# Deeper hi/lo rings, GpSimd alone on the ungated low halves, and expert cells fetched before expert rows, in a one-core PEER inference step

## What is computed

```python
q = (xb @ w_q).reshape(PEER_BLOCK, PEER_HEADS, 2, D_KEY // 2)      # 8 heads, two half keys of 128
s = jnp.einsum('thpc,pnc->thpn', q, sub_keys)
sv, si = lax.top_k(s, PEER_TOPK)                                   # 16 of 128, for each half
cand = sv[:, :, 0, :, None] + sv[:, :, 1, None, :]                 # 256 sums
best, flat = lax.top_k(cand, PEER_TOPK)                            # 16 of 256
idx = i1 * N_KEYS + i2                                             # one of 16384 experts
gate = jax.nn.softmax(best, axis=-1)
act = gelu(einsum('thkd,td->thk', u_tab[idx], xb))
coef = gate * act
out = einsum('thk,thkd->td', coef, v_tab[idx])                     # then x + out and a final RMSNorm
```

## Time and profile before

| | |
|---|---|
| median of 3 runs | 1560.5 us (1558.67 to 1567.8) |
| the profiled execution | 1566.55 us, its span 1564.7 us |
| queries | 501.8 to 575.5 us of the span |
| ungated blocks | to 829.4 |
| gated blocks | to 1112.2 |
| value stage | to 1556.0 |
| tail | to 1564.7 |
| TensorE matmul busy | 1372.6 us, 88% |
| VectorE, ScalarE, GpSimd busy | 64%, 43%, 23% |
| one pick on VectorE (line 1934, 128 x 1024), mean of 62 | 1278 ns |

### The profile page before, as it was taken

The page is one execution under the profiler, slowest core; times in us unless marked ns, Lnnn a source line. Parts: engine busy times, 40 slices in busy tenths (PEclk is TensorE's granted clock), DMA queues, the critical chain, the costliest instruction groups (busy, mean ns, idle before and its releaser), DMA issues.

```text
span 1564.7 us, 24623 instructions
## 1 busy us (share of the span) xinstructions
PE 1372.6 (88%) x8950; PEld 1177.7 (75%) x8950; DVE 1000.1 (64%) x1850; ACT 667.7 (43%) x1492; POOL 359.3 (23%) x284
## 2 busy tenths in 40 slices
PE   6999865998796998899999999999999159799997
PEld 5987632787434988889999999999877147677775
DVE  4556788444523248999327777777677147677776
ACT  4432042231002454344456666666555125455554
POOL 1110131001100015475661000000334743222210
PEclk9999676999888999999999999999999679999998
DMA  6430200000132334444546444444577158888864
GB/s 219 136 120 28 115 16 1 1 1 28 31 161 91 121 100 130 133 139 145 167 140 195 125 126 127 129 126 125 163 257 255 41 195 263 276 272 278 277 217 135
DMA packets 117612, 219.26 MB, mean 140 GB/s; under 512 B 31649, under 2 KB 32161, under 8 KB 116513
## 3 DMA queue, kind: packets, MB, share of 16 engines
q1 hardware_dynamic: 106272, 184.78, 37.5%
q0 software_dynamic: 11264, 33.60, 6.5%
HBM read 207.64 MB, written 10.42 MB: 139 GB/s over the span
## 4 chain that ended last, share of the span: by engine, by line
PE 41%; DVE 10%; POOL 7%; DMA 4%; issue 4%; ACT 3%; SPq 0%; ACTq 0%; DVEq 0%; POOLq 0%
PE ph L1702 9%; PE ph L1703 8%; PE ph L1704 8%; PE acc L1772 4%; POOL RT L1590 4%; PE pg L1753 4%; PE acc L1774 4%; PE acc L1773 4%; DVE ohx L1934 3%; POOL lo L1579 2%; ACT hi L1612 2%; DMA raw<-in_v 2%; DVE lo L1787 1%; DVE hid L1812 1%; DVE hid L1809 1%
## 5 line engine op out<-in xcount | busy, mean ns | idle before, releaser
L1612 ACT ACTIVATE hi<-raw 128x512 fp32r<-128x512 f32 x544 | 341.6, 632 | 483.0 <-PE acc L1774 203.2
L1787 DVE TENSOR_TENSOR lo<-raw,hi 128x512 fp32r<-128x512 f32 x448 | 313.7, 709 | 209.8 <-ACT hi L1612 208.2
L1702 PE MATMUL ph<-xh,hi 128*128 128x320 f32 x1152 | 366.4, 318 | 27.4 <-DVE lo L1787 20.8
L1703 PE MATMUL ph<-xl,hi 128*128 128x320 f32 x1152 | 358.1, 311 | 0.0
L1704 PE MATMUL ph<-xh,lo 128*128 128x320 f32 x1152 | 357.9, 311 | 0.0
L1772 PE MATMUL acc<-hi,ch 128*128 128x512 f32 x512 | 207.6, 405 | 74.8 <-DVE cl L1945 74.7
L1702 PEld LDWEIGHTS ph<-xh,hi 128*128 128x128 f32 x1152 | 218.5, 190 | 33.7 <-DVE lo L1787 22.9
L1703 PEld LDWEIGHTS ph<-xl,hi 128*128 128x128 f32 x1152 | 218.6, 190 | 0.0
L1704 PEld LDWEIGHTS ph<-xh,lo 128*128 128x128 f32 x1152 | 218.1, 189 | 0.0
L1774 PE MATMUL acc<-lo,ch 128*128 128x512 f32 x512 | 201.9, 394 | 0.0
L1773 PE MATMUL acc<-hi,cl 128*128 128x512 f32 x512 | 201.7, 394 | 0.0
(11 more groups left out here) (360 smaller groups left out, 1890.9 us busy)
## 6 DMA issues: line engine op xcount, KB each, us to landing
raw<-in_uT SPq DMA_DIRECT2D x256, 256.0 KB, 2.7
raw<-in_v SPq DMA_DIRECT2D x256, 256.0 KB, 3.1
wraw<-in_w_in SPq DMA_DIRECT2D x30, 512.0 KB, 3.5
raw<-in_w_q SPq DMA_DIRECT2D x32, 256.0 KB, 2.8
wo<-in_w_out SPq DMA_DIRECT2D x4, 1024.0 KB, 10.7
h_scratch<-act_s SPq DMA_DIRECT2D x128, 32.0 KB, 2.5
sth<-in_state_h SPq DMA_DIRECT2D x1, 2048.0 KB, 7.6
out_hgrn_s<-stn SPq DMA_DIRECT2D x1, 2048.0 KB, 6.9
```

The lines of the kernel that those rows point to most:

```text
L1612: act.activation(wide(hi[n % 4]), wide(raw[n % 4]), ACT.Copy).then_inc(t_hi, 1)
L1702: pe.matmul(o, hi[s][:, k], xh[:, c], start=begin, stop=False)
L1703: pe.matmul(o, hi[s][:, k], xl[:, c], start=False, stop=False)
L1787: dve.tensor_tensor(wide(lo[n % 4]), wide(raw[n % 4]), wide(hi[n % 4]), ALU.subtract).then_inc(lo_v, 1)
```

## The change

It does these things:

- `hi` and `lo` have 8 buffers each (`RING`); `raw` keeps 4. The four row buffers `vbuf` are no longer memory of their own, but the first 4096 columns of `hid`, free once the value stage has read its first 16 blocks (GpSimd waits for `c_lo` 16).
- ScalarE's `high` runs ahead by six tiles in place of two (`high(2m + 6)`, `high(UA + 2b + 6)`); in the value stage two blocks ahead.
- GpSimd makes all low halves of the ungated stage; `share()` is gone from the retrieval.
- ScalarE's loop over blocks is written in another order: `hidden(b-1)` comes first, then the scaling of the one-hots, then two `high`. The store of `act_s` moves from SP to ScalarE (`spill`), behind the two `high`.
- GpSimd fetches all 64 cells first and then the 64 sets of rows. `ACC_AT` is `38 + 4k/3`: three in four blocks, from block 38 to block 122. The steps of the tail move two blocks or one block later.
- The exponentials, the transposes of the picks and the loops of TensorE are placed by steps of 8 tiles in place of 4.

```diff
-        NPICK, EARLY = 64, 16
+        NPICK = 64
-        EXP_AT, PICKED = NA // 2 - 4, NA // 2 - 3
-        ACC_AT = {10 + 5 * k // 3: k for k in range(NPICK)}
+        RAW, RING = 4, 8
+        EXP_AT, PICKED = NA // 2 - 4, NA // 4 - 2
+        ACC_AT = {38 + 4 * k // 3: k for k in range(NPICK)}
...
-        vbuf = [big_mem.sb(f"vbuf{r}", [P, D]) for r in range(4)]
+        vbuf = [hflat[:, D * r:D * r + D] for r in range(4)]
...
-                    if n % 2 and 0 <= b < NBLK:
-                        sp.wait_ge(hs_done, b + 1)
-                        sp.dma_start(hs_dram[b], act_s[b % 4][:]).then_inc(hs_out[b % 4], 16)
...
-                    if n % 4 != 3:
-                        pool.wait_ge(t_hi, n + 1)
-                        pool.tensor_tensor(wide(lo[n % 4]), wide(raw[n % 4]), wide(hi[n % 4]), ALU.subtract).then_inc(lo_p, 1)
+                    pool.wait_ge(t_hi, n + 1)
+                    pool.tensor_tensor(wide(lo[n % RING]), wide(raw[n % 4]), wide(hi[n % RING]), ALU.subtract).then_inc(lo_p, 1)
...
-                for k in range(4):
-                    rows(k)
                 for r in range(4):
                     pool.wait_ge(hs_out[r], 16 * (NBLK // 4))
-                cells(0, 0, EARLY)
-                for k in range(4, EARLY):
-                    rows(k)
-                cells(1, EARLY, NPICK)
-                for k in range(EARLY, NPICK):
+                for k in range(NPICK):
+                    pool.indirect_dma_start(out=hsel[:, k:k + 1], out_offset=None, in_=hs_cells,
+                                            in_offset=bass.IndirectOffsetOnAxis(ap=cell_id[:, k:k + 1], axis=0)) \
+                        .then_inc(hsel_in, 16)
+                pool.wait_ge(c_lo, 4 * D // DT)
+                for k in range(NPICK):
                     rows(k)
...
                 def high(n):
                     act.wait_ge(t_in[n % 4], 16 * (n // 4 + 1))
-                    if n >= 4:
-                        act.wait_ge(t_mm, n - 3)
+                    if n >= RING:
+                        act.wait_ge(t_mm, n - RING + 1)
...
-                high(UA)
-                high(UA + 1)
+                def spill(b):
+                    act.wait_ge(hs_done, b + 1)
+                    act.dma_start(hs_dram[b], act_s[b % 4][:]).then_inc(hs_out[b % 4], 16)
+
                 for b in range(NBLK):
+                    if b:
+                        hidden(b - 1)
+                    if b == 2 * EXP_AT - 4:
+                        act.wait_ge(e_in, 3)
+                        act.activation(best_flat, best_flat, ACT.Exp).then_inc(e_out, 1)
                     if b >= NA:
                         g = b - NA
                         act.wait_ge(oh_raw, g + 1)
...
                         ins.then_inc(oh_ready, 1)
-                    high(UA + 2 * b + 2)
-                    high(UA + 2 * b + 3)
+                    high(UA + 2 * b + 6)
+                    high(UA + 2 * b + 7)
+                    if b:
+                        spill(b - 1)
...
-                    if b:
-                        hidden(b - 1)
 
                 for v in range(NBLK):
...
-                        low(UV + 2 * v + 2)
-                        if v == 0:
-                            times_hidden(NG - 1, NG)
-                        low(UV + 2 * v + 3)
+                    if v == 1:
+                        times_hidden(NG - 1, NG)
+                    if v < NBLK - 2:
+                        low(UV + 2 * v + 4)
+                        low(UV + 2 * v + 5)
                     if v in ACC_AT:
                         picked_row(ACC_AT[v])
```

More of the change, by code:

```diff
@@ L1503, in build_program @@
         v_in = [sem(f"v_in{r}") for r in range(4)]
-        hsel_in = [sem(f"hsel_in{r}") for r in range(2)]
+        hsel_in = sem("hsel_in")
         (keys_in, t_hi, lo_v, lo_p, t_mm, q_ready, s_full, s_ready, e_in, e_out, pk_ready, pt_full, rt_ready, ones_set,
@@ L1583, in rows @@
                         pool.wait_ge(v_used, k - 3)
[L1584 removed]
+                    pool.indirect_dma_start(out=vbuf[k % 4], out_offset=None, in_=v_rows,
                                             in_offset=bass.IndirectOffsetOnAxis(ap=row_id[:, k:k + 1], axis=0)) \
                         .then_inc(v_in[k % 4], 16)
[L1588 to L1592, removed]
                 pool.wait_ge(id_ready, 1)
[L1594 to L1596 removed]
                 for r in range(4):
                     pool.wait_ge(hs_out[r], 16 * (NBLK // 4))
[L1599 to L1603 removed]
+                for k in range(NPICK):
[4 more added lines that the diff above has]
+                for k in range(NPICK):
                     rows(k)
@@ L1619, in scores @@
                     act.activation(scs[half, 2 * (h % 4) + a], pss[half, m % 2, 2], ACT.Copy).then_inc(s_ready, 1)
+                for n in range(6):
+                    high(n)
                 for m in range(NQ + 1):
                     if m < NQ:
-                        high(2 * m)
-                        high(2 * m + 1)
+                        high(2 * m + 6)
+                        high(2 * m + 7)
                     if m >= 1:
@@ L1727, in step_a @@
                 def step_a(i, first):
-                    for u in range(4):
-                        if u % 2 == 0 and not first:
-                            pe.wait_ge(hs_done, 2 * i + (u // 2 - 1))
-                        if u < 3:
-                            pe.wait_ge(lo_p, 3 * i + (u + 1))
-                        else:
-                            pe.wait_ge(lo_v, i + (WQ + 1))
-                        unit(ph[:, u // 2, 0:NT], u, u % 2)
+                    for u in range(RING):
+                        if u % 2 == 0 and (u >= 4 or not first):
+                            pe.wait_ge(hs_done, 4 * i + (u // 2 - 1))
+                        pe.wait_ge(lo_p, 8 * i + (u + 1))
+                        unit(ph[:, u // 2 % 2, 0:NT], u, u % 2)
                 step_a(0, True)
@@ L1771, in step_v @@
                                 o, cols = acc[:, 2 * t + h], slice(P * t, P * t + P)
-                                pe.matmul(o, ch[c][:, cols], whi, start=first and c == 0, stop=False)
-                                pe.matmul(o, cl[c][:, cols], whi, start=False, stop=False)
-                                ins = pe.matmul(o, ch[c][:, cols], wlo, start=False, stop=last and c == 1)
+                                pe.matmul(o, ch[c % 2][:, cols], whi, start=first and c == 0, stop=False)
+                                pe.matmul(o, cl[c % 2][:, cols], whi, start=False, stop=False)
+                                ins = pe.matmul(o, ch[c % 2][:, cols], wlo, start=False, stop=last and c == 3)
                             ins.then_inc(t_mm, 1)
                 step_v(0, True, False)
-                with pe.Fori(1, NBLK // 2 - 1) as i:
+                with pe.Fori(1, NBLK // 4 - 1) as i:
                     step_v(i, False, False)
-                step_v(NBLK // 2 - 1, False, True)
+                step_v(NBLK // 4 - 1, False, True)
             @block.vector
@@ L1863, in _ @@
                     retrieve(PH, lambda g: sc[:, i, g], best[:, i], [picked[:, i, 0], picked[:, i, 1]])
-                assert shared[0] <= EXP_AT
-                while shared[0] < EXP_AT:
-                    share()
                 dve.wait_ge(e_out, 1)
@@ L1875, in _ @@
                     normalise(best[:, i], PH, picked[:, i, 2]).then_inc(pk_ready, 1)
-                while shared[0] <= PICKED:
-                    share()
                 dve.wait_ge(pt_full, 2)
@@ L1883, in _ @@
                 dve.memset(hflat[:, MID:LAST], 1.0).then_inc(ones_set, 1)
-                while shared[0] < NA // 2:
-                    share()
                 def one_hots(g):
```

120 lines of the change are left out of this document (50 added, 70 removed).

## The result

The changed kernel takes **1614.15 us** (median of 4 runs, 1608.01 to 1620.01), the kernel before 1559.59 in the same comparison (4 runs, 1550.04 to 1567.8): ratio 1.0352, 95% interval 1.028 to 1.0423. It is slower, by 55 us; 1604 was forecast, inside a range of 1572 to 1662. The profiled execution took 1608.01 us, its span is 1606.2, the shortest of its four.

A forecast was written before the change was run, and what follows sets the result against it. TensorE was taken as full in gated blocks, losing 28 us to waits and half clock in ungated ones, and stalled in the value stage. 1564.7 - 23 + 131 + 3 - 72 = 1603.7 us span, median 1604, range 1572 to 1662.

The forecast's parts named there:

- The gated step: Gated blocks: TensorE and ScalarE run one behind the other, losing 2.06 us a block, 131 us over 64 blocks.
- The rival of a short pass: Gated blocks: gelus begin sooner, under 1.8 us lost a block, so the gains win; 1540 us at 1.45; chance 0.10.
- The store on ScalarE: Gated blocks: act_s store costs ScalarE 0.43 us, 3.6 of 6.5 us used in all, so it costs nothing.
- The clock: Gated blocks: TensorE idle 28% of each period in short gaps; 3 us charged for clock drops.
- The rival (0.24): Gated blocks: gaps also drop the clock, 1.7 us in every second block, 54 us, giving 1655 us; chance 0.24.
- The ungated stage: Ungated blocks: waits for VectorE's low halves go and GpSimd keeps ahead; 230 us, a gain of 23.
- the rival in which GpSimd can't carry it: Ungated blocks: VectorE's retrieval slows GpSimd to 2.47 us a tile, 41 us more, 1645 us; chance 0.08.
- The value stage: Value stage: fetching cells first removes the 46.8 us stall; 372 us against 443.8, a gain of 72.
- I take 2.92: Value stage, 85 blocks carrying picks: 2.92 us each, between DMA-bound ends 2.74 and 3.27, 248 us.
- the 2 set down for restarts: Value stage: 2 us charged for restarts, beside 5 us for the load of the residual rows.
- best end of -89: Value stage: the largest gain in its range, 89 us, with pick blocks at 2.74 us.
- The start: Up to the end of the queries: no change, ending at 575.5 us as before.

The follow-up runs named there:

- e1: Changed kernel with ScalarE scaling a gated block's one-hots ahead of hidden(b-1) again, store of act_s left on ScalarE: 1481.51 us, ratio 0.9491.
- e2: Kernel before with only hidden(b-1) put ahead of the one-hot scaling in gated blocks: 1690.62 us, ratio 1.0844.
- e4: e1 with VectorE again making every fourth low half of the ungated stage between retrieval steps, rings of 8 kept: 1505.53 us, ratio 0.9655.
- e8: Kernel before with only GpSimd making all low halves of the ungated stage, rings of 4: 1542.75 us, ratio 0.9927.
- e3: e1 with 8 raw buffers from value block 64 on, the extra four in used blocks of hid: 1467.95 us, ratio 0.9415.
- e7: e3 with the 8 raw buffers from value block 36 on and the residual-row load issued in four pieces six blocks apart: 1450.9 us, ratio 0.9301.

## Why the prediction was right, and where it was off

**The gated step was right, mechanism and size.** The forecast added up the pass between two in-order engines from listed distances to 2.06 us a block; 1.99 was measured, in two kernels. e1 and e2 show the cause by taking it away and by putting it alone. Nearly all of the 0.07 too much is one term, ScalarE's reaction to the end of a matmul: 0.10 in the sum, 0.03 in the rows above (1001.95 + 0.31 = 1002.26, then 1002.29). The estimated hop back of 0.05 came out (1002.97 + 0.98 = 1003.95, then 1004.00). The rival of a short pass needed less than 1.8 us a block, and the row nearest to it, the one `pg` that waited, showed only the end of such a gap.

**The store on ScalarE** costs nothing, as forecast: the profile lists 0.33 us for its issue, and e1, which has it, runs the gated stage at TensorE's full rate.

**The clock** cost 3.4 us, forecast 3. The rival (0.24) that took the drop of the earlier trace rows for the pattern fell: 64 gaps of 1.74 us in periods of 6.41 brought two drops in the changed kernel. What the earlier trace rows has that these gaps lack isn't settled here.

**The ungated stage** came out at 229.9 us, forecast 230, and the rival in which GpSimd can't carry it fell: at 1.48 us a tile in the mean it stays under TensorE's 1.76. Two statements of the forecast hold only together, as e4 and e8 show: that VectorE's late low halves go, and that the ring hides GpSimd's slow ones. The forecast set the low halves of VectorE down at 13.7 us, their listed waits; e8 shows 11 of the stage's 22 us without the ring. What it did not see is that a late low half keeps its `raw` buffer, which by the waits of e4 and not by a run of its own is where a ring of 8 `hi` and `lo` doesn't help.

**The value stage was mis-sized**, -55 against -72, the term "I take 2.92" above all. The mechanism of its first half was right: no wait for the cells, 38 blocks in 103 us, the stall of 46.8 us gone. In the blocks with picks the forecast took a rate between two ends of bandwidth, 2.74 and 3.27, "nearer to the full-rate end because the bursts are spread over more buffers". The buffers that met the bursts were not more: a tile occupies one of 4 `raw` from the issue of its load until its low half, landing (4.74 and 6.42 us in the chain), copy 0.64, low half, and on VectorE often a pick in front. The rate measured is 3.06, 0.14 x 85 = 12 us more. The rest is the load of the residual rows. Its six blocks begin here and end at the 1410.20 shown above:

```profile
1380.94 0.42 ACT L1672 ACTIVATE ch<-hid 128x256 fp32r<-128x256 f32 x1 [0.89 <-PE acc L1765]
```

They took 1410.20 - 1380.94 = 29.3 us where six at 3.06 are 18.4: 11 us instead of 5. The 5 us are what the same load cost in the kernel before. The forecast didn't see that the change puts a wait of SP in front of it, as told at e3; that this wait makes the other 6 us is likely and not shown. 12 + 6 = 18, less the 2 set down for restarts, which the 29.3 already hold, makes the 16.5 us missing (388.5 - 372). `raw` was named in the forecast as a reason to stay above 2.74, and then not costed. The forecast's best end of -89 leaves out those same 2 us: with them its terms give -87.

The Trainium skill ("DMA: Bandwidth & Descriptors", section "Specifications") gives about 358 GB/s as a core's share of HBM, and the forecast worked out from it that TensorE's 2.72 us would bind, then set it aside for the trace's 281 GB/s. The runs bear out what was worked out from it: with 8 buffers TensorE's 2.72 us do bind, at 328 GB/s over 150 us. They don't bear out the figure as an upper limit of what this core moves, since e7 has 397 GB/s over 15 us. The 281 were what 4 buffers let through.

**The start** was assumed unchanged. The code there is the same in all kernels up to some 500 us, yet the queries (the same in before and e8) ended at 575.5 us in the profile of before, 565.4 after, 572.8 in e1, 569.5 in e4, 563 in e8. The changed kernel began them 12.0 us earlier than the kernel before (489.8 against 501.8) and took 1.9 us longer for them, so the 10 us are no gain of the change. Two executions of the same instructions up to there, before and e8, differ by 12 us, and the granted clock in the windows of the start differs with them:

```profile
0.00:502.00 502.00, 413.95 (x3345) 309.93 (x3346) 282.89 (x471) 133.96 (x233) 56.52 (x59) 0.88 0.20 72
```

```profile
0.00:490.00 490.00, 402.36 (x3348) 304.46 (x3349) 282.54 (x470) 133.58 (x232) 57.18 (x59) 0.91 0.21 74
```

So whole executions of these kernels, taken singly, can't be compared to better than that; stage by stage they can. This start was luck, and it hid an error: with the start of before, the span would have been 1616.3 against the forecast's 1603.7, 12.6 us more, which is 16.5 in the value stage less 4 in the stages ahead of it. The median of after lies 10 us above the forecast.

## What to carry to other kernels

Where two in-order engines hand work to each other, read the order of each stream for a cycle: if B's work on block b stands ahead of what A needs for block b+1, the overlap is gone whatever the depth of the rings, and its price can be added up from the listed distances before anything runs. A ring is only as deep as the shallowest one in the cycle. A load, its copy and its subtraction wait on `raw`: in the value stage 13 us are left for the doubled `hi` and `lo`, where four more `raw` behind all the picks, with the one large load spread out, gave 31 more. A wait that a load queue makes for anything but its own buffer stops every load behind it; look at such waits again when an engine moves ahead. A throughput read in a stretch where engines wait for landings is what the buffers let through; don't take it for a limit.

## What the runs showed of the hardware

- A TensorE that idled 1.74 us in every 6.41, for 410 us, kept 2.4 GHz nearly throughout: two drops that lost 1.7 us each in the changed kernel, a mean of 1.00 in e2.
- One core's DMA queues sustained 328 GB/s for 150 us at 0.94 busy (e3), 361 GB/s for 30 us at 1.00 and 397 GB/s for 15 us within these (e7).
- GpSimd's subtraction of a 128 x 512 tile took 1.48 us in the mean beside VectorE's retrieval, 1.29 alone.
- The same code up to the end of the queries took 575.5 us in one execution (before) and 563.0 in another (e8), at a mean granted clock of 0.88 and 0.91 in its first 500 us.
